# A two-layer hybrid decoder step on one Trainium2 core: the triangular inversion of the delta rule, written in 32x32 tiles

## The reference: what is computed

```python
decay = jnp.exp(jnp.where(incl, G[..., :, None] - G[..., None, :], -jnp.inf))
kk = jnp.einsum('nbhid,nbhjd->nbhij', kc, kc)
m = jnp.where(strict, bc[..., :, None] * kk * decay, 0.0)
a_mat = m + jnp.eye(CHUNK, dtype=m.dtype)
rhs = jnp.concatenate([vc * bc[..., None], kc * (bc * jnp.exp(G))[..., None]], axis=-1)
sol = lax.linalg.triangular_solve(a_mat, rhs, left_side=True, lower=True, unit_diagonal=True)
qk = jnp.einsum('nbhid,nbhjd->nbhij', qc, kc) * decay
def step(s, xs):
    u = w_n - jnp.einsum('bhck,bhkv->bhcv', kcd_n, s)
    o = jnp.einsum('bhck,bhkv->bhcv', qd_n, s) + jnp.einsum('bhij,bhjv->bhiv', qk_n, u)
    s = s * cd_n[..., None, None] + jnp.einsum('bhck,bhcv->bhkv', kt_n, u)
```

## Time and profile before

| what | value |
|---|---|
| time, median of 3 runs | 1540.61 us (1539.35 to 1540.62) |
| profiled execution, its own time | 1541.34 us |
| profiled execution, span from first to last instruction | 1539.7 us |
| PE busy | 1511.4 us (98%) |
| DVE busy | 561.1 us (36%) |
| ACT busy | 354.3 us (23%) |
| POOL busy | 59.6 us (4%) |
| mean granted TensorE clock | 0.997 of full speed |
| PE in the inversion levels (L2047, L2059, L2069), busy | 60.0 us |

### The profile page before, as it was taken

One profiled execution on the slowest core, in us unless ns is written; L12 is line 12 of the kernel. 1 busy time (PEld: TensorE's weight loads), 2 busy tenths in 40 slices (PEclk: granted clock), 3 DMA queues, 4 the chain that ended last, 5 costly groups with the idle time before them and its releaser, 6 DMA issues.

```text
span 1539.7 us, 32756 instructions
## 1 busy us (share of the span) xinstructions
PE 1511.4 (98%) x14439; PEld 1028.7 (67%) x14439; DVE 561.1 (36%) x944; ACT 354.3 (23%) x583; POOL 59.6 (4%) x100
## 2 busy tenths in 40 slices
PE   9999999899999999999999999999999999999998
PEld 8989888899999989834544544545445445445443
DVE  6767869666665577410111101101101101111113
ACT  6566544444444453300000000000000000000001
POOL 0000031000000000020000000000000000000010
PEclk9999999999999999999999999999999999999999
DMA  7764368254554575999999999999999999999992
GB/s 264 296 243 165 110 197 259 74 201 166 191 177 166 183 293 223 351 399 418 418 400 420 418 403 420 418 402 419 400 419 419 402 419 419 403 419 419 418 417 110
DMA packets 78052, 491.04 MB, mean 319 GB/s; under 512 B 9304, under 2 KB 9560, under 8 KB 53216
## 3 DMA queue, kind: packets, MB, share of 16 engines
q1 hardware_dynamic: 70000, 460.77, 75.2%
q0 software_dynamic: 7920, 28.25, 5.6%
HBM read 465.07 MB, written 23.92 MB: 318 GB/s over the span
## 4 chain that ended last, share of the span: by engine, by line
PE 88%; DVE 6%; ACT 3%; DMA 2%; issue 1%; SPq 0%; DVEq 0%; ACTq 0%
PE PP L2316 38%; PE PP L1746 22%; PE PP L2326 19%; DVE dlo L369 2%; ACT dhi L363 2%; PE PP L2059 1%; PE PP L2069 1%; DMA ring<-in_mkv 1%; PE PP L1864 1%; PE PP L1848 0%; PE PP L2199 0%; PE PP L1840 0%; PE PP L2047 0%; PE PP L1826 0%; DMA ring<-in_wi 0%
## 5 line engine op out<-in xcount | busy, mean ns | idle before, releaser
L2316 PE MATMUL PP<-ring,gen 128*32 128x448 f32 x6144 | 582.4, 539 | 1.8 <-DVE gen L1600 1.2
L2316 PEld LDWEIGHTS PP<-ring,gen 128*32 128x32 f32 x6144 | 270.9, 110 | 310.5 <-issue 308.6
L2326 PE MATMUL PP<-ring,gen 128*32 128x512 f32 x2688 | 293.3, 592 | 0.1
L2326 PEld LDWEIGHTS PP<-ring,gen 128*32 128x32 f32 x2688 | 150.4, 110 | 138.5 <-issue 138.3
L1746 PE MATMUL PP<-uh,dhi 128*128 128x264 f32 x736 | 213.2, 290 | 3.7 <-DVE dlo L369 2.9
L1684 DVE TENSOR_TENSOR gen<-ubuf,PP 128x448 f32<-128x448 f32 x48 | 26.9, 617 | 518.6 <-PE PP L2316 518.6
L369 DVE TENSOR_TENSOR dlo<-ring,dhi 128x2048 fp32r<-128x2048 f32 (+2 forms) x85 | 175.5, 2065 | 96.4 <-ACT dhi L363 96.0
L1746 PE MATMUL PP<-ul,dhi 128*128 128x264 f32 x736 | 208.8, 284 | 0.0
L1746 PE MATMUL PP<-uh,dlo 128*128 128x264 f32 x736 | 208.6, 283 | 0.0
L946 ACT ACTIVATE ubuf<-PP 128x448 f32<-128x448 f32 x48 | 22.6, 544 | 782.2 <-PE PP L2316 782.2
L363 ACT ACTIVATE dhi<-ring 128x2048 fp32r<-128x2048 f32 (+2 forms) x85 | 147.0, 1730 | 106.7 <-PE PP L1746 77.7
(11 more groups left out here) (453 smaller groups left out, 1365.5 us busy)
## 6 DMA issues: line engine op xcount, KB each, us to landing
ring<-in_w_up SPq DMA_DIRECT2D x256, 896.0 KB, 18.6
ring<-in_w_down SPq DMA_DIRECT2D x112, 1024.0 KB, 19.1
ring<-in_wi SPq DMA_DIRECT2D x22, 1024.0 KB, 4.8
ring<-in_a_in SPq DMA_DIRECT2D x18, 1024.0 KB, 4.8
ring<-in_wo SPq DMA_DIRECT2D x16, 704.0 KB, 4.1
slot_rows<-ring POOLq DMA_DIRECT2D x25, 384.0 KB, 15.6
ring<-in_mkv SPq DMA_DIRECT2D x8, 1024.0 KB, 5.2
ring<-in_kc SPq DMA_DIRECT2D x8, 1024.0 KB, 8.9
```

What stands on the lines that cost most here:

```text
L2316: mm = pe.matmul(bank((c // KD % 2) * SG + g)[SL * q:SL * (q + 1), 0:FQ], xs[:, at_:at_ + SL], w[:, q * FQ:(q + 1) * FQ], start=(k == 0), ...
L2326: return pe.matmul(out[SL * quarter:SL * (quarter + 1), :], hT[:, at_:at_ + SL], w[:, k * D + h * 512:k * D + (h + 1) * 512], start=(j == ...
```

## The change

- **Tiles.** M is inverted in its 32x32 diagonal blocks first (5 levels, `LV`; the first on DVE from `pairs`), for all 8 heads and 4 blocks in one set of small products (`blocks32`: 32 products of 32x32x32, each with its row group and column group of the array). Two more steps join pairs of blocks to 64 (`pair_y`, `pair_z`) and halves to 128 (`half_y`, `half_z`).
- **Compact forms.** The blocks of the inverse and of its transpose lie side by side in `TU` (128x512) and are both kept up to date by products, so nothing is transposed. Masks are 32 columns wide.
- **Strength in the decays.** ln(beta) is added to the negated cumulative decay (`cnG`), so `brow`, the scaling of M and that of v fall away.
- **Second solve.** `WT` is made from the decayed keys and the inverse before the state is known; the solve of chunk 1 accumulates both products in PSUM.
- **Sample states.** Fading is apart from adding: ACT fades parts 0 to 4 (`faded(k)`), POOL 5 to 7, DVE adds 512 columns at a time (`state_sum`). The outer products come in eight pairs `outer(k)`; POOL makes their right sides.
- **Queues.** POOL clears the expert rows between the projection tiles; SP loads the first two states two tiles earlier.

```diff
-                    sp.wait_ge(s("ain_mm"), 36)
                     for x in range(4):
+                        sp.wait_ge(s("ain_mm"), 34 if x < 2 else 36)
...
+            for i in range(NST + 1):
+                pool.wait_ge(s("ain_mm"), 9 + i)
+                pool.dma_start(step_rows[i]. ...
...
+            pool.wait_ge(s("sd_mm"), 1)
+            faded(FADES)
+            pool.wait_ge(s("sd_row"), 3)
+            pool.wait_ge(s("sd_cat"), 1)
+            for r in range(4):
+                pool.tensor_tensor(ublk[r]. ...).then_inc(s("sd_in"), 1)
...
+            for c in range(2):
+                pool.wait_ge(s("dl_tu"), 2 * (LV - 1) + c + 1)
+                for b in range(2):
+                    ins_ = pool.tensor_copy(heads128(Ub[c])[quad(b), :, quad(b)], heads32(TU[c][:, HALF:2 * HALF])[quad(b)])
+                ins_.then_inc(s("dl_ud"), 1)
+            pool.wait_ge(s("dl_ud"), 2)
+            for k in range(FADES + 1, 8):
+                faded(k)
+            pool.wait_ge(s("dl_eg"), 1)
+            pool.wait_ge(s("dl_kk"), 4)
+            pool.tensor_tensor(act[:, 0:H, P:SEQ], act[:, 0:H, P:SEQ], heads128(eg), ALU.mult).then_inc(s("dl_qd"), 1)
...
+            def faded(k):
+                for g in groups(k):
+                    for q in range(4):
+                        n = 16 * (k // 2) + 4 * q + g
+                        ins_ = a.activation(state[:, n * P:(n + 1) * P], state[:, n * P:(n + 1) * P], ACT.Copy, scale=sgb[:, n:n + 1])
+                    ins_.then_inc(s("faded"), 1)
...
+            for c in range(2):
+                a.wait_ge(s("dl_y"), 2 * (LV - 1) + c + 1)
+                a.activation(Y64[c], bank(5 - 2 * c)[:, 0:HALF], ACT.Copy).then_inc(s("dl_ev"), 1)
+            faded(3)
...
+            for c in range(2):
+                a.wait_ge(s("dl_y"), 2 * LV + c + 1)
+                a.activation(Y128[c][64:128], bank(5 - 2 * c)[64:128, :], ACT.Copy).then_inc(s("dl_ev"), 1)
+            faded(4)
...
+            def state_sum(k):
+                for i, g in enumerate(groups(k)):
+                    v.wait_ge(s("sd_outer"), 2 * k + i + 1)
+                    if k < FADES:
+                        v.wait_ge(s("faded"), 2 * k + i + 1)
+                    else:
+                        v.wait_ge(s("faded_late"), 2 * (k - FADES) + i + 1)
+                    v.tensor_tensor(state_part(k, g), state_part(k, g), heads128(bank(6 + i)), ALU.add).then_inc(s("state_new"), 1)
...
+            def blocks32(out, left, right):
+                for x in range(H):
+                    for b in range(4):
+                        mm = pe.matmul(out[quad(b), quad(x)], left(x, b), right(x, b), start=True, stop=True)
+                return mm
...
+            def step_y(lv, c):
+                pe.wait_ge(s("dl_tu"), 2 * (lv - 1) + c + 1)
+                blocks32(bank(5 - 2 * c)[:, 0:HALF], key_block(c), block_of(TU[c])).then_inc(s("dl_y"), 1)
+
+            def step_z(lv, c):
+                pe.wait_ge(s("dl_ym"), 2 * (lv - 1) + c + 1)
+                blocks32(bank(4 - 2 * c)[:, 0:HALF], block_of(TU[c], HALF), block_of(Y32[c]))
+                blocks32(bank(4 - 2 * c)[:, HALF:2 * HALF], block_of(Y32[c]), block_of(TU[c], HALF)).then_inc(s("dl_z"), 1)
...
+            def outer(k):
+                pe.wait_ge(s("sd_in"), k // 2 + 2)
+                if k == 0:
+                    pe.wait_ge(s("sd_cat"), 1)
+                else:
+                    pe.wait_ge(s("state_new"), 2 * k)
+                for i, g in enumerate(groups(k)):
+                    pe.matmul(bank(6 + i), krow[quad(g), :], ublk[k // 2][quad(g), :], start=True, stop=True).then_inc(s("sd_outer"), 1)
...
+            for x in range(H):
+                mm = pe.matmul(PP[0][:, head(x)], kdec[:, head(x)], Ub[1][:, head(x)], start=True, stop=True)
+            mm.then_inc(s("dl_tok"), 1)
...
+                pe.matmul(PP[1][:, head(x)], Ub[1][:, head(x)], vtok[1][:, head(x)], start=True, stop=False)
+                mm = pe.matmul(PP[1][:, head(x)], WT[:, head(x)], Sb[:, head(x)], start=False, stop=True)
```

More of the change, by code:

```diff
@@ L1318, in _ @@
[L1318 to L1334 removed]
+            v.wait_ge(s("conv_state"), 2)
@@ L1972, in gram @@
                 mm.then_inc(s("dl_kk"), 1)
-            def brow(c, out):
-                for x in range(H):
-                    mm = pe.matmul(out[:, head(x)], gb[:, c, x:x + 1].to_broadcast([P, P]), ident, start=True, stop=True)
-                mm.then_inc(s("dl_brow"), 1)
             def tokens(c, m0, out):
@@ L2005, in _ @@
-            gram(1, 8, PP[1])
-            pe.wait_ge(s("dl_neg"), 2)
-            pe.wait_ge(s("dl_eg"), 2)
-            brow(1, PP[2])
-            pe.wait_ge(s("dl_pt"), 2)
-            tokens(1, 16, PP[3])
+            step_y(1, 1)
+            step_z(1, 0)
+            pe.wait_ge(s("ain_out"), 36)
+            pe.wait_ge(s("sd_in"), 1)
+            pe.wait_ge(s("state_loaded"), 32)
+            for n in range(DBH):
+                g = n % 4
+                if n == DBH // 2:
+                    pe.wait_ge(s("state_late"), 32)
+                mm = pe.matmul(bank(6)[32 * g:32 * g + 32, 0:P], kq_diag[:, 32 * n:32 * (n + 1)], state[:, n * P:(n + 1) * P],
+                               start=(n < 4), stop=(n >= DBH - 4))
@@ L2011, in _ @@
+            mm.then_inc(s("sd_mm"), 1)
+            pe.matmul(bank(7)[:, 0:64], ones[:, :], kqd, start=True, stop=True)
+            pe.transpose(bank(7)[:, P:2 * P], kpad, ident).then_inc(s("sd_rows"), 1)
+            step_z(1, 1)
+            step_y(2, 0)
             pe.wait_ge(s("dl_kt"), 1)
             tokens(1, 8, PP[0])
[L2014 to L2020 removed]
@@ L2095, in head_sums @@
+            step_y(4, 0)
+            step_y(4, 1)
+            outer(2)
+            step_z(4, 0)
+            step_z(4, 1)
+            outer(3)
+            pair_y(0)
+            pair_y(1)
+            outer(4)
+            pair_z(0)
+            pair_z(1)
+            half_y(0)
+            half_y(1)
+            outer(5)
+            half_z(0)
+            half_z(1)
             def head_sums(c, out, at_, n):
@@ L2101, in head_sums @@
                 mm.then_inc(s("on_mm"), 1)
-            solve(0, vtok[0])
-            pe.wait_ge(s("state_new"), 14)
-            state_step(0, PP[2])
-            pe.wait_ge(s("state_new"), 16)
-            result(0, PP[3])
+            pe.wait_ge(s("dl_un"), 3)
+            pe.wait_ge(s("dl_ud"), 1)
+            for x in range(H):
+                mm = pe.matmul(PP[2][:, head(x)], Ub[0][:, head(x)], vtok[0][:, head(x)], start=True, stop=True)
+                if x % 4 == 3:
+                    mm.then_inc(s("dl_uu"), 1)
@@ new lines, in _ @@
+            outer(6)
+            pe.wait_ge(s("dl_un"), 4)
+            pe.wait_ge(s("dl_ud"), 2)
+            pe.wait_ge(s("dl_pt"), 2)
+            for x in range(H):
+                mm = pe.matmul(PP[0][:, head(x)], kdec[:, head(x)], Ub[1][:, head(x)], start=True, stop=True)
+            mm.then_inc(s("dl_tok"), 1)
+            for x in range(H):
+                pe.wait_ge(s("dl_u"), x // 4 + 1)
+                mm = pe.matmul(PP[2][:, head(x)], ktail[0][:, head(x)], wrow[0][:, head(x)], start=True, stop=True)
```

540 lines of the change are left out of this document (292 added, 248 removed).

## The result

The changed kernel takes 1554.68 us (median of 4 runs, 1553.89 to 1555.88), the kernel before 1539.98 beside it. The ratio is 1.0102, 95% interval 1.009 to 1.0114. The prediction was 1527, with a range up to 1548: wrong in sign. Profiled execution: span 1553.3 against 1539.7.

A forecast was written before the change was run, and what follows sets the result against it. PE was taken to bound the kernel: 27.1 us gained up to the first solve, 6.9 given back after, 20.1 net, less 3.8 for clock and 2.5 for changes of form, 13.8; 1527 against 1540.61, range 1514 to 1548.

The forecast's parts named there:

- The small products, the term that decides: 28 `blocks32` sets of 64 passes on PE before the first solve, 0.65 us each, 18.2 us.
- passes at the sustained rate: Rival, 15%: each 32x32 pass costs 27.4 ns, a set 1.75 us; the walk ends 13.5 us later than before, 1555.
- The pair steps: `pair_y` and `pair_z` on PE before the first solve: 0.65 us and 1.3 us each, summed to 3.9 us.
- Up to the first solve: From PE's first decay product: 55.8 us of work and 11.5 of waits; first solve at 256.5, 27.1 us earlier.
- Waits: PE's waits before the first solve, on ACT, DVE and the faded states: 11.5 us in all.
- The clock: Lower PE clock after the waits at `outer(4)` and `outer(5)`: 2 x 1.9 = 3.8 us lost.
- the clock stays at the low level through the tiled stretch: Rival, 8%: PE's thinly used array keeps the clock low, sets at 1.3 us; slower by 9 us, 1550.
- The outer products: Six pairs on PE before the first solve, four passes each at 0.53 us, 3.2 us in all.
- The fades: PE idles while ACT fades states: 4.5 us before `outer(4)` and 3.9 before `outer(5)`.
- The tail: From the first solve to the last head-norm product: 33 us instead of 26, giving back 6.9 us.
- POOL at nothing: POOL's new arithmetic costed at nothing: ready in time at twice the memset rate; at eight times the gain falls by 7.
- The same distances after it: Sign: after the last head-norm product, the trace keeps the distances of the kernel before.

The follow-up runs named there:

- fades_first: The changed kernel with faded(3) and faded(4) on ACT ahead of the copies of the 32-blocks, not behind the Y64 and Y128 copies; 1549.05 us (1.0055).
- with_full: The changed kernel with 56 further full products of constants, two in each set of small products, results not used; 1569.98 us (1.0182).
- tail_order: The changed kernel with the steps after the first solve in another order on ACT, DVE and PE; 1551.56 us (1.0063).
- burst_late: The kernel before with 256 extra 32x32 passes in one row in the last level, results not used; 1542.83 us (1.003).
- turned_blocks: The changed kernel with transposed blocks made by a DVE transpose instead of a second set of products, 18 sets instead of 28; 1536.44 us (0.9961).
- spread_256: The kernel before with 256 extra 32x32 passes, 32 behind each half of full products in level 1, results not used; 1552.38 us (1.008).

## Why the prediction was wrong

**The step that failed** is in "The small products, the term that decides": 0.65 us a set, "the burst rate, ... with a third for gaps in the fetch". The passes themselves came near it: 28 sets took 20.45 us in the chain, 0.73 each (11.4 ns a pass), 0.61 to 0.66 at full clock and 0.93 to 0.97 at 1.2 GHz. The fetch was mis-sized. I took 1.08 us a packet, which is how long the packet's own transfer lasts, for the time from one packet to the next. That is 3.5 to 4.0 us with idle DMA engines, and I shared all engines' instructions among the packets where PE's alone fill them (128 passes a packet, not 143). With the 18.0 us of gaps a set costs 1.37, about the 1.35 at which the forecast had the gain turn; what makes a loss of it is the clock and the outer products. 3.5 us for 128 passes are 27.3 ns each: the rival "passes at the sustained rate" (15%) has nearly the same number, for a mechanism that the starts 9 ns apart refute. That it also named 1555 is luck. The pair steps are summed wrongly in the prediction: their 160 passes are two and a half sets, 1.6 us by its own unit and not 3.9, and at the rival's price 4.4 and not 10.4, by which the rival comes to 1549. The rival also has no price for the clock.

**Up to the first solve**, 292.98 instead of 256.5. Start 1.0 later (a tile at a lower clock, 4.64 instead of 3.11). Gaps 17.9 in the chain. PE's work 77.6 instead of 55.8, by lines of the chain: outer products 10.0 for 3.2, half steps 7.2 for 3.4, grams and decay products 14.3 for 10.7, state products and neighbours 6.9 for 4.1, sets 20.5 for 18.2, pair steps 4.9 (at 1.2 GHz) for 3.9, the rest 13.9 for 12.3. Waits 7.8 instead of 11.5. Sum 37.0, of which 0.5 are the solve's own first product.

**The clock** is most of that second item. 38.2 us of PE's work before the solve lie in stretches at 1.2 GHz; at most half of it, 19.1, is its price. I had 3.8, for two waits. PE stopped eleven more times for instructions, and the rival "the clock stays at the low level through the tiled stretch" (8%) came true in part. In `fades_first` the clock stays low for 19.11 us in which PE never stops, so thin use of the array is enough to keep it down. Which of the two brings it down these runs don't part: `with_full` takes both away, and stays at 1.00.

**The outer products** were mis-sized without the clock too. Eight passes, on four row groups, took 1.07. Four passes on two groups take, at full clock,

```profile
260.18 1.07 PE PP L2139 x4
```

as long: six pairs, 3.2 us more than the forecast. So the four groups ran side by side, and half of them save nothing.

**The fades**: right. 4.5 and 3.9 us were forecast, 3.8 and 4.0 came, with 2.45 of ACT in each. `fades_first` shows that nothing else was hidden in them. The 1.9 us of clock that I added for each are not seen here, since the clock is at 1.2 GHz from 267.0 on, before the first of them; in `with_full` it does fall with the first of the two.

```profile
270.80 0.38 ACT ring L874
...
271.21 2.45 ACT ring L850 x8
...
273.75 0.70 DVE ring L1366
...
274.59 2.08 PE PP L2139 x4
```

**The tail**: 33.2 forecast, 34.87 came, and 1.9 of that is the solve at half speed. Right (though its nine terms add up to 14.7 and not to 14.8), and the cause fits: `tail_order`, which changes both orders that the prediction named, among others, takes 5.9 of it back.

**POOL at nothing**: right. No wait of PE or DVE in the delta rule ends on it. The decayed q took 2.35 us for 1024 columns, 2.3 ns each, 2.6 times the memset rate:

```profile
L599 POOL TENSOR_TENSOR ring<-ring,gen 128x1024 f32<-128x1024 f32 x1 | 2.3, 2347 | 0.0
```

The Trainium skill ("GPSIMD Engine Reference", 3.1 Elementwise) has about 2.6 cycles an element for a two-input operation, by the prediction's estimate 2.2 ns; the trace agrees.

**"The same distances after it"**: right but for 1.1 us in the dense products and the 3.3 of the execution.

**Open**: whether stops or thin use first bring the clock down; how a block's delay grows with DMA load; whether before's product form for the upper levels, mixed with fewer sets, would be better still.

## What to carry to other kernels

Count instructions, not only time: where PE uses up 256 in less than 3.5 to 4 us (two per pass, so over 128 short passes in a row), it waits for the next block, and the share of the fetch queue (0.5%) shows nothing of it; "issue" gaps that cut a loop in the middle do. Put long products between short ones, or let another engine make what a second set would. And a stop can be paid twice, since full products behind it may run at 1.2 GHz, and a long stretch of small products stays there even without a stop: price a chain of short steps with its stops and its clock before its work.

## What the runs showed of the hardware

Small passes on four diagonal 32x32 tiles start 8.5 ns apart over 199 passes (`burst_late`). Blocks of 256 instructions follow each other at 3.5 to 3.7 us with idle DMA engines in the changed kernel and at 4.0 in `turned_blocks` (PE goes on at 223.43, 227.44 and 231.45, DMA share 0.02); at a DMA share of 1.00 one took over 6.8 (`spread_256`). PE busy without a break for 19.11 us on small and thin products was granted 1.2 GHz throughout (`fades_first`). A 32x32 transpose of 256 columns on DVE takes 0.45 us, less than the 0.73 of the set that it replaces. 35.3 us of extra full products between the small ones made the stretch 11.7 longer (`with_full`).
